# Moving the staging ring 64 bytes down in on-chip memory, with its four split weight buffers 0, 32, 32 and 64 bytes further up in it

## The reference

```
kv = RMSNorm(mem) @ w_mkv
z  = RMSNorm(x) @ w_in                    # u | v | p | q | three gate fields
A  = gelu(u) * (tril(W_s) @ LayerNorm(gelu(v)) + b_s)
B  = (trailing means of p - p) @ w_pool * scale
C  = attention(q, kv)
x  = x + (sum_i sigmoid(gate_i) * (branch_i @ w_br_i)) @ w_o
x  = x + MoE(RMSNorm(x))                  # top-1 of 4 groups, top-2 of its 8 SwiGLU experts
y  = RMSNorm(x)
```

## Time and profile before

| | |
|---|---|
| median of 3 runs | 1586.09 us (1585.43 to 1587.51) |
| the profiled execution | 1585.38 us, its span 1583.6 us |
| TensorE, VectorE, ScalarE busy | 1349.8, 556.1, 407.4 us |
| moved from HBM | 540.30 MB |

### The profile page before, as it was taken

The page is one execution under the profiler, slowest core; times in us unless marked ns, Lnnn a source line. Parts: engine busy times, 40 slices in busy tenths (PEclk is TensorE's granted clock), DMA queues, the critical chain, the costliest instruction groups (busy, mean ns, idle before and its releaser), DMA issues.

```text
span 1583.6 us, 24065 instructions
## 1 busy us (share of the span) xinstructions
PE 1349.8 (85%) x9971; PEld 920.1 (58%) x9971; DVE 556.1 (35%) x898; ACT 407.4 (26%) x623; POOL 19.9 (1%) x54
## 2 busy tenths in 40 slices
PE   9999999999999999999778578488487497497597
PEld 8999999999999999963222232232232232232231
DVE  6657765554455555432112012012021021021024
ACT  6545343333333344332102002002002002002003
POOL 0000000000000000010000000000000000000000
PEclk9999999999999999999989789789789699699699
DMA  9777445545555669799999999999999999999997
GB/s 364 291 273 280 158 160 187 186 159 193 180 184 185 260 235 388 283 398 427 437 433 440 432 426 441 432 427 442 432 428 440 430 430 439 430 430 439 427 430 301
DMA packets 42425, 544.68 MB, mean 344 GB/s; under 512 B 5753, under 2 KB 7929, under 8 KB 13697
## 3 DMA queue, kind: packets, MB, share of 16 engines
q1 hardware_dynamic: 42088, 543.96, 83.8%
q10 hardware_dynamic: 288, 0.04, 0.0%
HBM read 540.30 MB, written 3.68 MB: 343 GB/s over the span
## 4 chain that ended last, share of the span: by engine, by line
PE 69%; DMA 28%; ACT 1%; DVE 1%; issue 0%; SPq 0%; ACTq 0%; DVEq 0%
DMA ring<-in_expert_chunks 28%; PE bank L1653 12%; PE bank L1654 12%; PE bank L1655 12%; PE bank L2125 8%; PE bank L2122 6%; PE bank L2039 5%; PE bank L1980 3%; PE bank L2025 1%; ACT side L1087 1%; PE bank L2031 1%; PE bank L1972 1%; PE bank L2115 1%; PE bank L2027 1%; PE bank L1912 1%
## 5 line engine op out<-in xcount | busy, mean ns | idle before, releaser
L1142 DVE TENSOR_TENSOR w_lo<-ring,w_hi 128x1024 fp32r<-128x1024 f32 x216 | 255.9, 1226 | 224.8 <-ACT w_hi L845 224.2
L1653 PE MATMUL bank<-xn_hi,w_hi 128*128 128x264 f32 x1120 | 319.0, 285 | 0.0
L1654 PE MATMUL bank<-xn_lo,w_hi 128*128 128x264 f32 x1120 | 317.3, 283 | 0.0
L1655 PE MATMUL bank<-xn_hi,w_lo 128*128 128x264 f32 x1120 | 317.1, 283 | 0.0
L845 ACT ACTIVATE w_hi<-ring 128x1024 fp32r<-128x1024 f32 x216 | 217.1, 1052 | 373.6 <-PE bank L1655 313.9
L2122 PE MATMUL bank<-side 128*32 128x512 f32 x1024 | 131.4, 651 | 97.0 <-DMA side<-in_expert_chunks 96.8
L1653 PEld LDWEIGHTS bank<-xn_hi,w_hi 128*128 128x128 f32 x1120 | 210.9, 188 | 1.7 <-issue 1.4
L1654 PEld LDWEIGHTS bank<-xn_lo,w_hi 128*128 128x128 f32 x1120 | 211.1, 188 | 0.1
L1655 PEld LDWEIGHTS bank<-xn_hi,w_lo 128*128 128x128 f32 x1120 | 210.0, 187 | 0.0
L2122 PE MATMUL bank<-ring,side 128*32 128x512 f32 x752 | 102.4, 667 | 86.4 <-DMA ring<-in_expert_chunks 86.4
L1553 DVE TENSOR_SCALAR side<-bank,small 128x128 f32<-128x128 f32 x56 | 19.6, 351 | 369.7 <-PE bank L1980 369.7
(11 more groups left out here) (333 smaller groups left out, 1581.5 us busy)
## 6 DMA issues: line engine op xcount, KB each, us to landing
ring<-in_dense_units SPq DMA_DIRECT2D x108, 1024.0 KB, 4.8
ring<-in_expert_chunks SPq DMA_DIRECT2D x21, 4096.0 KB, 22.5
trunk<-in_expert_chunks SPq DMA_DIRECT2D x13, 4096.0 KB, 35.0
ring<-in_expert_chunks SPq DMA_DIRECT2D x20, 2048.0 KB, 16.2
ring<-in_expert_chunks SPq DMA_DIRECT2D x17, 1024.0 KB, 18.2
side<-in_expert_chunks SPq DMA_DIRECT2D x4, 4096.0 KB, 29.6
side<-in_expert_chunks SPq DMA_DIRECT2D x5, 2048.0 KB, 11.3
trunk<-in_expert_chunks SPq DMA_DIRECT2D x5, 2048.0 KB, 16.3
```

The lines of the kernel that those rows point to most:

```text
L1142: V.tensor_tensor(w_lo[n % 2][:, js, :], raw[n % 2][:, js, :], w_hi[n % 2][:, js, :], ALU.subtract).then_inc(lo_done, 1)
L1653: mm(ps[:, 0:n], w_hi[b][:, j, :], x_hi[:, j, :], start=j == k0, stop=False)
L1654: mm(ps[:, 0:n], w_hi[b][:, j, :], x_lo[:, j, :], start=False, stop=False)
L1655: ins = mm(ps[:, 0:n], w_lo[b][:, j, :], x_hi[:, j, :], start=False, stop=j == k1 - 1)
```

## The change

The `lead` padding in front of the ring, 64 bytes, is dropped, and the ring starts there and is 64 bytes longer. So everything behind the ring keeps its address. What starts at the ring's start or at a fixed distance from it (`raw`, `xn_lo`, the two expert places, the small `thr2` and `npf`) moves 64 bytes down. The four weight buffers get their own shifts inside the ring: `w_hi[0]` 0, `w_lo[0]` 32, `w_hi[1]` 32 and `w_lo[1]` 64 bytes. No instruction, transfer, wait or size changes.

```diff
-LINE = 256
+RING0 = 16
+PLACE0 = 0
+W_PAD = ((0, 8), (8, 16))
...
-        arena = -(-start // LINE) * LINE
-        if arena > start:
-            sb("lead", (arena - start) // 4)
-        ring = sb("ring", 4 * CHUNK + P)
+        arena = start
+        ring = sb("ring", RING0 + 4 * CHUNK + P)
...
-        TRUNK0 = 4 * CHUNK + P + 3 * D
+        TRUNK0 = RING0 + 4 * CHUNK + P + 3 * D
...
-        w_hi = [split_part(f"w_hi{b}", UNIT0 + b * CHUNK, KT * P).rearrange("p (j c) -> p j c", j=KT) for b in range(2)]
-        w_lo = [split_part(f"w_lo{b}", UNIT0 + b * CHUNK + KT * P, KT * P).rearrange("p (j c) -> p j c", j=KT)
-                for b in range(2)]
+        w_hi, w_lo = [[split_part(f"w_{name}{b}", UNIT0 + b * CHUNK + i * KT * P + W_PAD[b][i], KT * P).rearrange("p (j c) -> p j c", j=KT)
+                       for b in range(2)] for i, name in enumerate(("hi", "lo"))]
...
-        pair = [view(ring, 0, 2 * CHUNK), view(ring, 2 * CHUNK, 2 * CHUNK), view(trunk, 0, 2 * CHUNK),
+        pair = [view(ring, PLACE0, 2 * CHUNK), view(ring, PLACE0 + 2 * CHUNK, 2 * CHUNK), view(trunk, 0, 2 * CHUNK),
...
-        thr2 = view(ring, 4 * CHUNK, 9)
-        npf = view(ring, 4 * CHUNK + 9, 2)
-        quad = {0: view(side, 4352, 4 * CHUNK), 2: view(ring, 0, 4 * CHUNK)}
+        thr2 = view(ring, PLACE0 + 4 * CHUNK, 9)
+        npf = view(ring, PLACE0 + 4 * CHUNK + 9, 2)
+        quad = {0: view(side, 4352, 4 * CHUNK), 2: view(ring, PLACE0, 4 * CHUNK)}
```

## The result

The changed kernel takes 1592.24 us (median of 4, 1590.88 to 1593.15) beside 1585.76 us before: ratio 1.0038, 95% interval 1.0026 to 1.005. That is 4 to 8 us slower, where 4 us faster was forecast. The profiled execution's span is 1589.7 us, 6.1 us over that of before.

The account below looks back on a forecast made before the run. TensorE was taken to bound the dense part and transfers the expert part. Terms -4.2 (TensorE) + 0 + 0 + 0 from the median 1586.1 gave 1581.9, so 1582 us; own range 1579 to 1584, over all 1575 to 1590.

Parts of the forecast that it names:

- The bound and the way through: Dense part bound by TensorE, expert part by transfers; dense microseconds saved pass to the end one for one.
- the address modulo 256 bytes sets the cost: Dense products: moving against stationary address sets the cost, 129 ns at worst, 116 to 118.5 at the five best positions.
- a plain shift permutes the costs: On `xn` and `br`, shifting all alike only reorders the 24 costs and leaves 120.9 ns.
- TensorE, terms of the sum: Dense part's 5088 products: 0.8 ns less each, -4.2 us; ends kept at -12 and +4.1 us.
- the five positions over 122 ns: Dear places among 24 products on `xn` and `br`; coming down to the middle saves 19.9 ns per 24.
- Rival B: Dense part: unlike relations for high and low parts slow TensorE, +2.9 to +6 us, 1589 to 1592 us; chance 0.18.
- uniform in the way of 2j+2: On `mg`, all three products of a block get one relation; in the slower-TensorE case 0.8 ns better, -0.6 us.
- The transfers: Loads into the ring, starting 192 bytes past a multiple of 256: 0 taken, upper end 4.2 us.
- The argument from the earlier trace: The `wp` load already started 192 bytes off; its packets paid at most 8 ns, fixed part included.
- ScalarE and VectorE: Their work on the same buffers stays under TensorE even at 10% either way: 0, with 0.1 us either way.
- TensorE in the expert part: Reading chunks at another residue may change it, but 217 us of idle in 780 cover several per cent: 0.
- Rival B's switch: On `xn` units, a mean distance over 121.6 ns decides for slower TensorE.

Follow-up runs that it names:

- plain: Kernel before with the ring and all in it 64 bytes down, the four weight buffers without shifts of their own; ratio to before 1.0019.
- ring_only: Changed kernel with weight buffers and `xn_lo` put back where they stood; only `raw` and the expert places 64 bytes down; ratio to before 1.0007.
- map_dma: Rest of the step left out, only transfers into on-chip memory at chosen starts; twenty queued 1 MB transfers: 50.1 us at 0, 50.6 us at 192 bytes.
- The map: Rest of the step left out, only TensorE's products at freely chosen starts; 1056-byte blocks: equal starts 120.8 to 120.9 ns, 59 of 63 others 121.1 to 123.3.
- after: The changed kernel itself, against the kernel before; 1592.24 us, ratio 1.0038.
- All three maps: Three runs of TensorE's products alone, varying starts, then product order, block order and distance, then two layouts in turn; equal starts 120.8 ns in each.

## Why the prediction was wrong

**The bound and the way through** were right: TensorE sets the dense part, and its 5.36 us reach the end of the program with 0.7 us more.

**That the address modulo 256 bytes sets the cost** of a product was right, and so was that a plain shift permutes the costs on `xn` and `br`: 120.8 ns at all eight common shifts alone on the engine, and on `br` in plain. On `mg` it was not so: plain took 122.2 instead of 121.7 ns.

**The step that failed** is the choice inside "TensorE, terms of the sum": that the five positions over 122 ns come down to the middle because they arise where all three products stand in the same bad relation, -0.8 ns a product and -4.2 us. The dearest product of the `xn` units went from 129 to 125 (parity 0) and 128 ns (parity 1), but the calm ones of 116 to 118.5 ns went too, down to none at parity 0, and on `br` there are now products of 129 and 132 ns. In place of -0.8 the mean rose by 0.8 on `xn` (1.0 with the units at the upper level) and by 0.8 and 1.8 on `br`. The equal relation wasn't the fault of the layout but nearly its best case; 59 of 63 ways to leave it came out dearer. I had read the dear positions and left out that the cheap ones come from the same relation.

**Rival B** (unlike relations cost, `mg` as the sign of it) had the sign and about the size: +2.9 to +6 us against 5.4. Its sizes by part were about right for `xn` and `br` (0.8 ns foretold, 0.8 to 1.8 found); on `mg` a gain of 0.8 ns was foretold, and 0 and 0.5 ns were lost at the two parities, so that "uniform in the way of 2j+2" isn't what `mg` lacked. That the sum fits is in part luck: a gain that didn't come stands against products and transfers that B hadn't counted. `mem` got 2.2 ns cheaper rather than dearer, worth at most 0.4 us. The 96 products with 512 moving columns I had not costed at all; they hold 0.6 us.

**The transfers** were set to 0 with an upper end of 4.2 us; by the packets' times 0.9 us is lost over 675 of some 880 us of stream, about 1.2 in all as an estimate, and the timed runs of ring_only allow up to 2.5. The argument from the earlier trace rows failed at one point: `wp` was one load with nothing queued behind it, and single loads don't pay in map_dma either. By the Trainium skill ("DMA: Bandwidth & Descriptors", "How a descriptor splits into AXI transactions") every descriptor off 256 bytes would pay, and the estimate was 7 ns; 8 KB packets pay 4.6 ns in the expert stream and none when they come singly, 64 KB packets 0.2 ns as a mean over ring and `side`.

**ScalarE and VectorE** at 0 was right (1054 and 1225 ns, and ring_only). **TensorE in the expert part** stayed hidden.

Rival B's switch (mean distance over 121.6 ns on `xn`) was crossed at 121.7.

What stays open: why the relation matters inside the chip. The map orders the layouts and doesn't explain them; that the weight load and the moving stream disturb each other is the only reading of the rows that I have, and it was argued, not shown. Nor is it shown why a unit falls to the one or to the other of its levels, or which queued transfers pay for their start and which don't. The changed placement was only tried at the shifts named; `xn_lo` at 0 with spread weights was not tried in the whole kernel, where only `br` stands so, and is in the map alone.

## What to carry to other kernels

Before moving a stationary or moving operand, count its start modulo 256 bytes against its partners': where the moving blocks walk through the residues, as on `xn` and `br`, buffers that take part in the same run of products should share one, and the price of leaving it is here about 1 ns in 121, too small for one product's row and 5 us over 5000 products. Where all blocks stand at one residue, as on `mem`, sharing is no rule: there equal starts gave 120.0 ns and another shift 113.3 and 117.8. A pattern of dear and cheap positions is an average to be compared as an average; taking only the dear ones down is not a forecast. And a load that was cheap alone says nothing of the same load in a full queue.

## What the runs showed of the hardware that was not expected

- The distance of back-to-back fp32r products (128x128 weights) depends on the addresses even with no other engine running: 113.3 to 120.0 ns for 256 columns at eight constant relations, 120.0 to 122.2 for 264, 226.7 to 234.3 for 512.
- The same layout has more than one value (121.7 and 122.4 ns on `xn` in after, in a turn of units that TensorE alone repeats). `mg` in plain (122.2 against 121.7 at permuted relations) may be a case of it.
- A destination off 256 bytes slows an 8 KB packet from 312 to 315 or 316 ns on average when twenty transfers are queued, about equally at 32, 64, 128 and 192 bytes, and not at all when they come one at a time or in turn with 4 MB transfers; at 64 KB it is 0.2 to 4 ns of 2418.
- With the Trainium skill ("TensorE: Matmul & The Clock Gate", "Step-by-step: what each phase is for") TensorE's two read ports are independent. All three maps speak against taking that as "addresses don't matter".
